# One program without stage barriers, two weight tiles ahead of each norm's root, and dense tokens in blocks of 32 tokens by 4 heads

## What is computed

```python
for layer in range(2):
    hn = rms_norm(h, mixer_norm[layer])
    h = h + (mla_mixer(hn) if layer == 0 else rglru_mixer(hn))
    h = h + peer_ffn(rms_norm(h, ffn_norm[layer]))
out = rms_norm(h, final_norm)[:, 16:]

def rms_norm(x, g):
    return x * rsqrt(mean(x * x, -1) + 1e-6) * g

def peer_ffn(x):                                  # 8 heads, 128 x 128 keys
    q = (x @ w_query).reshape(-1, 8, 2, 128)
    s = einsum('thpd,pkd->thpk', q, sub_keys)     # 2 x 128 scores a head
    sv, si = top_k(s, 16)                         # then the best 16 of the 256 pairs
    top_s, eidx = best 16 of sv[0] + sv[1]
    w = softmax(top_s) * gelu(einsum('thkd,td->thk', u_tab[eidx], x))
    return einsum('thk,thkd->td', w, v_tab[eidx])

def rglru_mixer(h):
    gate, xr = gelu(h @ w_in[:, :1024]), h @ w_in[:, 1024:]
    xc = causal 4-tap convolution of xr
    a, b = functions of sigmoid(xc @ w_a + b_a) and sigmoid(xc @ w_x + b_x)
    return (linear scan of a, b over the tokens * gate) @ w_out
```

## Time and profile before

| | |
|---|---|
| median of 3 runs | 1637.57 us (1636.19 to 1637.85) |
| profiled execution, its own time | 1636.25 us |
| its span | 1634.5 us |
| TensorE (PE) busy | 1599.5 us, 98% |
| VectorE (DVE) busy | 1090.1 us, 67% |
| ScalarE (ACT) busy | 212.6 us, 13% |
| GpSimd (POOL) busy | 498.9 us, 31% |
| moved by DMA | 534.97 MB, mean 327 GB/s |
| granted TensorE clock, mean | 0.997 |

### The profile page before, as it was taken

One profiled execution on the slowest core, in us unless ns is written; L12 is line 12 of the kernel. 1 busy time (PEld: TensorE's weight loads), 2 busy tenths in 40 slices (PEclk: granted clock), 3 DMA queues, 4 the chain that ended last, 5 costly groups with the idle time before them and its releaser, 6 DMA issues. The chain is left out here.

```text
span 1634.5 us, 30408 instructions
## 1 busy us (share of the span) xinstructions
PE 1599.5 (98%) x12244; PEld 1517.5 (93%) x12244; DVE 1090.1 (67%) x2433; ACT 212.6 (13%) x617; POOL 498.9 (31%) x423
## 2 busy tenths in 40 slices
PE   9999999999899999999999999999999999999997
PEld 7687899999899999998898888999999999999997
DVE  3362369998899998545436423999969989943441
ACT  2251221111011000000003312211211100000000
POOL 0000033336444456533300001233534434532310
PEclk9999999999999999999999999999999999999999
DMA  6303379999999999999983435899999999999991
GB/s 242 129 15 132 124 279 394 395 384 402 408 409 408 399 408 408 409 409 409 409 316 133 140 123 193 328 396 393 383 409 408 408 406 403 409 409 410 408 383 64
DMA packets 149981, 534.97 MB, mean 327 GB/s; under 512 B 17617, under 2 KB 20434, under 8 KB 149842
## 3 DMA queue, kind: packets, MB, share of 16 engines
q1 hardware_dynamic: 89938, 314.90, 50.2%
q0 software_dynamic: 59904, 218.13, 33.9%
...
## 5 line engine op out<-in xcount | busy, mean ns | idle before, releaser
L243 PE MATMUL ps<-big,raw 128*128 128x160 f32 (+2 forms) x5232 | 830.9, 320 | 3.4 <-ACT big L1131 3.1
L243 PEld LDWEIGHTS ps<-big,raw 128*128 128x128 f32 x5232 | 775.8, 191 | 43.9 <-issue 3.8
L1067 PE MATMUL ps<-big,raw 128*128 128x160 f32 x4096 | 579.0, 301 | 7.0 <-DVE big L1062 2.6
L1067 PEld LDWEIGHTS ps<-big,raw 128*128 128x128 f32 x4096 | 559.6, 190 | 16.2 <-DMA raw<-in_v_rows 12.9
L1091 POOL DMA_INDIRECT big<-in_u_rows,big x208 | 253.6, 1219 | 751.6 <-DVE big L1201 397.9
L1232 DVE SCALAR_TENSOR_TENSOR big<-big 128x1024 f32<-128x1024 f32 x201 | 258.0, 1284 | 190.5 <-PE ps L1067 114.5
L1091 POOL DMA_INDIRECT big<-in_v_rows,big x208 | 242.1, 1164 | 318.6 <-DVE big L1232 246.8
L1215 DVE CUSTOM_DVE_ANT_0 big<-big 128x1024 f32<-128x1024 f32 x208 | 244.3, 1221 | 24.1 <-DMA big<-in_u_rows,big 17.5
L1131 ACT ACTIVATE big<-ps 128x160 f32<-128x160 f32 x256 | 77.6, 304 | 512.2 <-PE ps L243 463.8
L1161 DVE MAX8 big<-big 128x8 f32<-128x128 f32 (+1 forms) x99 | 33.5, 339 | 103.0 <-ACT big L1100 91.1
L331 ACT ACTIVATE big<-h 128x272 f32<-128x272 f32 (+1 forms) x32 | 12.7, 420 | 647.5 <-DVE h L1306 597.3
...
## 6 DMA issues: line engine op xcount, KB each, us to landing
raw<-in_u SPq DMA_DIRECT2D x256, 512.0 KB
raw<-in_v_rows SPq DMA_DIRECT2D x256, 512.0 KB
...
big<-in_u_rows,big POOLq DMA_INDIRECT x208
big<-in_v_rows,big POOLq DMA_INDIRECT x208
```

Source lines behind the costliest of these rows:

```text
L243: mm = pe.matmul(out, w[:, c * P:(c + 1) * P], x[:, c, :], start=(c == 0), stop=(c == DC - 1))
L1067: return pe.matmul(accumulator(c), w, act_w[:, i, :], start=start, stop=False, skip_group_check=True)
```

## The change

It has four parts.

1. **One block.** The stages return their programs (`Part`) and `trunk` runs them one after the other in one block, with no clearing and no meeting between stages. What one stage has to know of the one before, it gets from semaphores: `prior.summed`, `joined`, `updated`, `lead_ready`. The last `keep_busy` of each stage and the first of the next are gone, and the one at the program's start is shorter (36 for 48, and the 14 behind it gone).
2. **Two tiles ahead (LEAD = 2).** The root is one number per token, so it can be applied after the product. h times the gain alone (`gain_chunk`, `lead`) is multiplied with tiles 0 and 1 of the next stage, around the matmul of the sum of squares, and VectorE multiplies those two products by the root as it copies them out (`take_lead`). The copies of tiles 0 and 1 move from ACT to VectorE.
3. **Dense groups of 32 tokens by 4 heads.** DB = 5 blocks, again 10 groups in each layer. The first 5 can be scored at the ninth query tile. The finds go in another order, (first half of gathered), (first half of dense), (second half of gathered), (second half of dense), which makes 10 finds where there were 9 (layer 0) and 8 (layer 1): 3 of one group in layer 0 (1 before), 4 of one group in layer 1 (none before). Query products take one ACT copy less each, and the masks of the spread are half as wide.
4. **RG-LRU without meta tokens where they are not read.** The gate tiles and the output tiles are multiplied for 256 tokens, not 272.

```diff
+LEAD = 2
 class Stream:
+    def lead(self, pe, n, x, ready, first, last):
+        if first == 0:
+            self.wait_landed(pe, n)
+            pe.wait_ge(self.free[n % 2], n // 2 + 1)
+        for c in range(first, last):
+            if n == 0:
+                pe.wait_ge(ready, c + 1)
+            mm = pe.matmul(self.bank(n), self.tile(n)[:, c * P:(c + 1) * P], x[:, c, :], start=(c == 0),
+                           stop=(c == DC - 1), skip_group_check=True)
...
 class NextSum:
+    def gain_chunk(self, dve, c):
+        dve.wait_ge(self.updated, c + 1)
+        dve.tensor_scalar(self.lead[:, c, :], self.src[:, c, :], self.mem.vec[:, self.gain + c:self.gain + c + 1], None,
+                          ALU.mult).then_inc(self.lead_ready, 1)
...
 def mla
+        mem.tiles.fetch(sp, 0, LEAD)
-            norm.square_half(act)
-            act.wait_ge(consts_in, 48)
+        norm.square_all(act)
+        act.wait_ge(consts_in, 32)
...
+        for c in range(DC):
+            dve.tensor_scalar(lead[:, c, :], mem.h[:, c, :], mem.vec[:, VEC["mix0"] + c:VEC["mix0"] + c + 1], None,
+                              ALU.mult).then_inc(gained, 1)
+        norm.fold_squares(dve)
...
-            keep_busy(pe, mem, 6, 48)
+        keep_busy(pe, mem, 6, 36)
+        down.lead(pe, 0, lead, gained, 0, DC)
             norm.add_up(pe)
+        down.lead(pe, 1, lead, gained, 0, DC)
...
-            keep_busy(pe, mem, 6, 14)
-            next_sum.add_gathered(pe)
 def rglru
+        take_lead(0)
             convolve(0)
+        take_lead(1)
...
-            keep_busy(pe, mem, 6, 14)
+        prior.wait_banks(pe, 0)
+        st.lead(pe, 0, prior.lead, prior.lead_ready, 0, 2)
+        prior.add(pe, DC - 2).then_inc(st.done, 2)
+        prior.add(pe, DC - 1)
+        st.lead(pe, 0, prior.lead, prior.lead_ready, 2, DC)
+        prior.wait_banks(pe, 1)
+        st.lead(pe, 1, prior.lead, prior.lead_ready, 0, DC)
-            for n in range(2 * DC):
-                st.multiply_raw(pe, n, st.bank(n), xn, norm.scaled if n == 0 else None)
+        for n in range(LEAD, 2 * DC):
+            if n < DC:
+                st.multiply_raw(pe, n, st.bank(n), xn, norm.scaled if n == LEAD else None)
+            else:
+                st.multiply_raw(pe, n, st.bank(n)[:, 0:SEQ], xn[:, :, META:L])
...
-                st.multiply_raw(pe, n, st.bank(n), b, states if n == OUT else None)
+            st.multiply_raw(pe, n, st.bank(n)[:, 0:SEQ], b[:, :, META:L], states if n == OUT else None)
 def peer
-    GB, GD, NG = TG // LANES, TD // GT, TD // ST
+    GB, DB, NG = TG // LANES, TD // LANES, TD // ST
+    GD = DB * PH // HEADS_ABREAST
+    first_half = [*range(GB), *range(GG, GG + DB)]
+    second_half = [*range(GB, GG), *range(GG + DB, G)]
+    order = first_half + second_half
+    finds = (pairs_of(0, GB) + pairs_of(GG, GG + DB) + pairs_of(GB, GG) + pairs_of(GG + DB, G))
...
+        sp.wait_ge(prior.summed, 1)
...
-                act.copy(qt[:, s % 2, :, n // 2:n // 2 + 1, :].rearrange("p g a t -> p g (a t)"),
-                         mem.ps[:, s % 2, 0:TD].rearrange("p (g t) -> p g t", t=GT))
...
+        def take_lead(n):
+            st.wait_product(dve, n)
+            if EXTRA:
+                dve.tensor_tensor(qx[:, n, 0, :], mem.ps[:, n, TB:T], rstd[:, TB:T], ALU.mult)
+            dve.tensor_tensor(qg[:, n, :, 0, :], mem.ps[:, n, 0:TB].rearrange("p (b t) -> p b t", t=LANES),
+                              rstd[:, 0:TB].rearrange("p (b t) -> p b t", t=LANES),
+                              ALU.mult).then_inc(st.free[n], 1)
+        norm.wait_root(dve)
+        take_lead(0)
             norm.scale(dve, xn)
+        take_lead(1)
...
-            for first in range(0, G, 2):
-                find(first, min(2, G - first))
-                if first:
+        for k, (first, w) in enumerate(finds):
+            find(first, w)
+            if k:
                     n = rows(n, n + ROWS_PER_FIND)
...
-            by_head = [P, GD, PH, TOPK]
+        by_head = [P, GD, HEADS_ABREAST, TOPK]
...
-            keep_busy(pe, mem, TURN_BANK, 24)
+        prior.wait_banks(pe, 0)
+        st.lead(pe, 0, prior.lead, prior.lead_ready, 0, DC)
+        prior.add_gathered(pe)
+        prior.wait_banks(pe, 1)
+        st.lead(pe, 1, prior.lead, prior.lead_ready, 0, DC)
             pe.wait_ge(keys_in, 32)
```

More of the change, by code:

```diff
@@ L169, in __init__, with lead @@
         self.ps = ctx.enter_context(nc.psum_tensor("ps", [P, 8, 512], F32))
+    def lead(self, tokens):
+        return self.take(BIG, (DC, tokens))[0]
     def take(self, at, shape):
@@ L260, with __init__ @@
 class Norm:
-    def __init__(self, nc, ctx, mem, name, src, chunks, gain, squares, rstd, bank, tokens, given=False):
+    def __init__(self, nc, ctx, mem, name, src, chunks, gain, squares, rstd, bank, tokens, prior=None):
         def sem(what):
@@ L318, with __init__ @@
 class NextSum:
-    def __init__(self, ctx, mem, name, src, squares, tokens, bank=SUM_BANK):
-        self.mem, self.src, self.squares = mem, src, squares
+    def __init__(self, ctx, mem, name, src, squares, tokens, bank=SUM_BANK, gain=None):
+        self.mem, self.src, self.squares, self.gain = mem, src, squares, gain
+        self.lead, self.lead_ready = mem.lead(tokens), ctx.sem(f"{name}_lead_ready")
+        self.summed = ctx.sem(f"{name}_summed")
         self.sum = mem.ps[:, bank, 0:tokens]
@@ L730, in rglru @@
     xn, at = take(0, (DC, L))
-    gate, at = take(at, (DC, L))
+    gate, at = take(at, (DC, SEQ))
     xp, at = take(at, (DC, L + CONV - 1))
@@ L909, in sem, with peer @@
+    return part, next_sum
+def peer(nc, ctx, mem, d, layer, prior):
     def sem(name):
@@ L1020, in fold_at @@
         return mem.ps[:, bank, at:at + DC * width].rearrange("p (c t) -> p c t", t=width)
-    next_sum = NextSum(ctx, mem, f"peer{layer}_next", h, take(0, (DC, T))[0], T, PEER_SUM_BANK)
+    next_sum = NextSum(ctx, mem, f"peer{layer}_next", h, take(0, (DC, T))[0], T, PEER_SUM_BANK, gain=VEC["mix1"])
+    next_sum.banks_read = [(joined, COPIES), (joined, COPIES)]
     def products(pe, half, m):
```

1468 lines of the change are left out of this document (773 added, 695 removed).

## The result

The changed kernel takes 1620.47 us (median of 4 runs, 1619.69 to 1622.54) against 1637.35 us before (median of 4): the ratio is 0.9904, 95% interval 0.9893 to 0.9916. That is 16.9 us less where 22.3 were forecast, inside the stated range of 1604 to 1626 us. The profiled execution took 1619.69 us with a span of 1617.5.

A forecast was written before the change was run, and what follows sets the result against it. TensorE, busy 98% of the span, was taken to bound the kernel, with DMA a second limit in layer 0 only. Stage changes, start, last norm and narrower tiles 22.7 + 1.9 - 6.8 + 4.5 = 22.3 us off 1637.57: 1615, range 1604 to 1626.

The forecast's parts named there:

- Stage changes: Between stages: gains of 6.0 us from `mla` to `peer`, 5.8 from `rglru` to `peer`, 3.3 from `peer` to `rglru`.
- the narrower tiles: RG-LRU's gate and output tiles: 16 tiles at 256 tokens for 272, 0.20 us less each, gain 3.4 us.
- rival D: Stage changes: the root is late and a third tile waits, 2 to 3 us each; 1624 us, chance 0.06.
- Rival E: Stage changes: idle TensorE would start each stage at 1.2 GHz, 1.5 us lost each; 1621 us, chance 0.05.
- Start: First stage: tile 0 starts sooner and tile 2 at 17.8 us for 21.2, gain 3.4 us.
- the gains and the tile's landing let tile 0 start at about 8: First stage: tile 0 could start at about 8 us, where it started at 13.88 before.
- Last norm: At the last norm: without the meeting Ln starts at 1625.9 us for 1626.68, gain 0.8 us.
- Finds, layer 0: Layer 0's finds and first `hots`: `shifted` and the rows come 1.9 us sooner, gain 1.9 us, bounds 0 and 5.
- TensorE just waits longer there: Layer 0's first `hots`: TensorE's stall of 4.55 us grows to 4.55 - 1.9 + about 5, 7 to 8 us.
- v tiles: Layer 0's v tiles: 72 rows left for 78, fewer late tiles, gain 4.5 us, bounds 0 and 7.7.
- what is buffered lasted 29 tiles ... so 38 at 0.23: Layer 0 from v tile 40: buffered tiles last 38 tiles for 29, so 9 of 43 late tiles fewer, 2.7 us.
- Finds, layer 1: Layer 1's finds: the chain ends 9 us later, TensorE waits 5.3 us plus 1.5 of clock, loss 6.8 us.

The follow-up runs named there:

- e5: Changed kernel, but at the start of both peer layers TensorE does the sum and waits for the root before query tiles 0 and 1: 1630.2 us.
- e10: e5 with constant tiles in its two waits at the start of each peer layer, 18 ahead of the sum and 9 behind it: 1628.0 us.
- e1: Changed kernel with the old order of finds, all groups that look up rows first, then all dense groups, in pairs wherever possible: 1616.4 us.
- e7: Changed kernel with 12 of layer 0's 224 row transfers fetching 128 and not 1024 numbers per partition: 1618.3 us.
- e8: e2 with the last rows spread up to v tile 124 and not 118: 1611.3 us.
- e11: Changed kernel with 6 rows for 9 at each of the two places behind the finds: 1613.4 us.
- e12: Changed kernel with the first weight tile asked for ahead of the gains: 1619.3 us in one execution.
- e3: Changed kernel with constant tiles in two waits of layer 0, 56 before the first products and 14 before the first v tile: 1619.3 us.
- e2: Changed kernel with its order of finds kept in kind, but groups paired over the halves' border, so fewer finds: 1610.1 us.

## Why the prediction was right, and where it was off

**Stage changes: right.** 6.0, 5.8, 3.3 and 3.4 us (the narrower tiles) were measured as 6.0, 6.0, 3.3 and 3.4, and no tile 2 waited (rival D out). Its reason holds too, with more detail than it had: e5 and e10 split the gain. Rival E's clock loss is real where TensorE idles (e5), and the lead tiles prevent it.

**Start: 3.4 forecast, 2.1 measured.** The step "the gains and the tile's landing let tile 0 start at about 8" failed: the tile lands at 9.09, and the gains would not have been there at 8 either: where TensorE waited for them (e1, e7, e8, e11, e12) it began between 9.05 and 9.90.

**Last norm: 0.8 forecast, none at the end.** Ln comes 2.26 us behind the start of the last sum, not 3.09, as forecast. ACT and the stores after:

```profile
1608.74 0.47 ACT L340 ACTIVATE big<-ps,con 128x256 f32<-128x256 f32 x1 [0.98 <-PE ps L403]
...
1610.21 3.78 SPq L1562 DMA_DIRECT2D out<-big  x8
```

From the first store to the end of the span it is 7.3 us, against 6.35 before; what takes longer there the trace doesn't tell.

**Finds, layer 0: sign and size right up to the first products, 2.3 for 1.9, then 3.4 us lost that no term had.** The failed step is "TensorE just waits longer there": the sum priced the longer stall, but kept its clock as that of the shorter one. By e3 the dip costs 3.1 us in this trace, and the before kernel's 1.3; a second, behind 1.87 us at the first v tile, costs 1.7, of which v tiles would have waited for most anyway.

**v tiles: 4.5 forecast, 0.7 measured.** The step "what is buffered lasted 29 tiles ... so 38 at 0.23" failed. Waits of the weight loads for v tiles (us, times), before from 717 to 806 us and after from 712 to 799:

```profile
  DMA raw<-in_v_rows: 12.9, 35
...
  DMA raw<-in_v_rows: 11.9, 32
  issue: 0.4, 1
```

So tiles 77 to 111 were late before and 79 to 111 after, each 2.56 us for 2.17. The mean of 2.48 in the earlier trace rows is 8 tiles on time and 35 late, not 43 late by 0.30. Two late tiles fewer, by 0.38, are the 0.7 us measured. Why not more: the DMA queues of the rows (q0) and of the tiles (q1) from v tile 40 to 78, packets, MB and share, before (83.3 us) and after (82.5 us):

```profile
q0 software_dynamic: 4679, 17.04, 51.3%
q1 hardware_dynamic: 4649, 16.93, 50.9%
...
q0 software_dynamic: 4642, 16.92, 51.3%
q1 hardware_dynamic: 4600, 16.74, 51.0%
```

Each queue gets a half, 0.85 of a transfer for each tile that TensorE multiplies. Rows were asked for at 1.00 a tile before and at 0.92 after, and both are more than 0.85: the rows' queue takes its half either way, and the tiles in the ring, some six ahead at v tile 40 in both (an estimate from the bytes moved), go down by 0.15 a tile in both. The prediction drained the ring by all that was asked for, 0.30 and 0.23. VectorE in the changed kernel:

```profile
729.07 1.28 DVE L1351 SCALAR_TENSOR_TENSOR big<-big 128x1024 f32<-128x1024 f32 x1 [1.26 <-DMA big<-in_v_rows,big]
731.64 1.29 DVE L1351 SCALAR_TENSOR_TENSOR big<-big 128x1024 f32<-128x1024 f32 x1 [1.28 <-DMA big<-in_v_rows,big]
```

A row and a tile arrive each 2.56 us, the even share that the prediction had. By that the trace agrees with the rule of the Trainium skill (DMA: Bandwidth & Descriptors, Queues, rings and completion order) that engines go round between queues with work.

**Finds, layer 1: -6.8 forecast, -3.4 measured.** The stall is 1.70 for 5.3 us and no dip follows. VectorE's chain from the first find (973.02) to the products took 232.1 us, 1.3 less than forecast. TensorE was there 2.3 later than forecast, as the split scores make it wait 1.60 and 0.91 us for ACT and the spread matmuls take 1.78 for 1.40. What the stall seemed to spare was lost ahead of it. e1 and e2 show the mechanism: with pairs for singles the stall is gone.

In sum the order of the finds buys nothing, since it pays for the wait it fills with three or four single finds (8.7 to 9.2 us where a half of a pair is 7.35) and one or two more helpings of six rows. e2 fills the wait without them.

The total lay inside the range partly by luck. The start, the last norm, the dips of layer 0 and the v tiles came out 9 us worse than forecast together, and layer 1, where the stall and its dip were overrated, 3.4 better.
